# Last head's extra rows behind three known own rows, spread over three groups; 17 row dots per head instead of 16

## What is computed

```
q = (hc @ wq) -> [token, 8 heads, 2, 128];  sc = q . keys        (128 keys per half)
s1,i1 = top_k(sc[...,0], 16); s2,i2 = top_k(sc[...,1], 16)
top,pos = top_k(s1[:,None] + s2[None,:], 16); eidx = i1*128 + i2; gate = softmax(top)
act = gelu(u_tab[eidx] . hc);   out = sum_k (gate * act) * v_tab[eidx]
```

## Time and profile before

| what | value |
|---|---|
| median of 3 runs | 3503.8 us (3500.09 to 3504.2) |
| the profiled execution | 3505.83 us |
| its span | 3504.1 us |
| PE, DVE busy | 3398.9 us (97%), 2943.3 us (84%) |
| ACT, POOL busy | 1369.3 us (39%), 958.6 us (27%) |

### The profile page before, as it was taken

One profiled execution on the slowest core, in us unless ns is written; L12 is line 12 of the kernel. 1 busy time (PEld: TensorE's weight loads), 2 busy tenths in 40 slices (PEclk: granted clock), 3 DMA queues, 4 the chain that ended last, 5 costly groups with the idle time before them and its releaser, 6 DMA issues. The chain is left out here.

```text
span 3504.1 us, 67960 instructions
## 1 busy us (share of the span) xinstructions
PE 3398.9 (97%) x27550; PEld 3113.1 (89%) x27550; DVE 2943.3 (84%) x5651; ACT 1369.3 (39%) x2116; POOL 958.6 (27%) x756
## 2 busy tenths in 40 slices
PE   8899899999999999999999989999999999999998
PEld 5678777899999999999997877789999999999997
DVE  8687574899999978888888757489999997888887
ACT  3542353433334443333344234343333444333333
POOL 2000000044453333444510000003445333333352
PEclk9999999999999999999999999999999999999999
DMA  7830432499999999999962043249999999999995
GB/s 233 295 105 28 128 121 67 148 327 344 325 377 311 347 317 348 379 381 377 368 229 84 12 131 111 76 131 334 347 321 376 313 349 317 365 378 384 375 365 203
DMA packets 392169, 922.19 MB, mean 263 GB/s; under 512 B 33968, under 2 KB 211248, under 8 KB 385072
## 3 DMA queue, kind: packets, MB, share of 16 engines
q1 hardware_dynamic: 298672, 582.20, 48.6%
q0 software_dynamic: 93184, 335.65, 25.4%
HBM read 802.51 MB, written 113.05 MB: 261 GB/s over the span
## 5 line engine op out<-in xcount | busy, mean ns | idle before, releaser
L2570 POOL DMA_INDIRECT row<-in_peer_u_rows,row_at x320 | 424.4, 1326 | 654.2 <-DVE row L2908 574.3
L228 PE MATMUL peer_ps<-peer_h_high,tile_high 128*128 128x352 f32 (+1 forms) x1504 | 496.4, 330 | 6.3 <-DVE tile_low L221 6.2
L229 PE MATMUL peer_ps<-peer_h_low,tile_high 128*128 128x352 f32 (+1 forms) x1504 | 492.1, 327 | 0.0
L230 PE MATMUL peer_ps<-peer_h_high,tile_low 128*128 128x352 f32 (+1 forms) x1504 | 491.5, 327 | 0.0
L221 DVE TENSOR_TENSOR tile_low<-peer_tile,tile_high 128x1024 fp32r<-128x1024 f32 x362 | 439.6, 1215 | 27.2 <-ACT tile_high L216 26.9
L228 PE MATMUL peer_ps<-gate_high,tile_high 128*128 128x352 f32 x1360 | 441.0, 324 | 2.4 <-DVE tile_low L221 2.3
L230 PE MATMUL peer_ps<-gate_high,tile_low 128*128 128x352 f32 x1360 | 441.5, 325 | 0.0
L229 PE MATMUL peer_ps<-gate_low,tile_high 128*128 128x352 f32 x1360 | 439.6, 323 | 0.0
L216 ACT ACTIVATE tile_high<-peer_tile 128x1024 fp32r<-128x1024 f32 x362 | 379.8, 1050 | 80.6 <-DMA peer_tile<-in_peer_u 75.6
L216 ACT ACTIVATE gate_high<-weighed 128x352 fp32r<-128x352 f32 x256 | 127.8, 499 | 619.0 <-DMA peer_tile<-in_peer_v 301.8
L2908 DVE SCALAR_TENSOR_TENSOR row<-row,h_own 128x1024 f32<-128x1024 f32 x256 | 308.7, 1218 | 14.7 <-DMA row<-in_peer_u_rows,row_at 14.6
(11 more groups left out here) (569 smaller groups left out, 8042.7 us busy)
## 6 DMA issues: line engine op xcount, KB each, us to landing
peer_tile<-in_peer_u SPq DMA_DIRECT2D x256, 512.0 KB, 6.3
peer_tile<-in_peer_v SPq DMA_DIRECT2D x256, 512.0 KB, 6.2
gates<-gates_out SPq DMA_DIRECT2D x44, 1024.0 KB, 9.1
gates_in<-gates SPq DMA_DIRECT2D x32, 1408.0 KB, 10.0
acts<-up_act SPq DMA_DIRECT2D x220, 176.0 KB, 6.9
act_in<-acts SPq DMA_DIRECT2D x220, 176.0 KB, 6.4
in_w<-in_w_in SPq DMA_DIRECT2D x32, 512.0 KB, 3.6
peer_tile<-in_peer_wq SPq DMA_DIRECT2D x32, 512.0 KB, 4.5
```

What stands on the lines that cost most here:

```text
L228: pe.matmul(out, wh, mh, start=first, stop=False)
L229: pe.matmul(out, wh, ml, start=False, stop=False)
L230: return pe.matmul(out, wl, mh, start=False, stop=last)
L2570: pool.indirect_dma_start(row_of(n)[:, :], None, table, bass.IndirectOffsetOnAxis(ap=row_at[:, row_col(n):row_col(n) + 1], axis=0)) \
```

## The change

It sets `ROWS_BY_HEAD` to 17, `ROWS_BY_TILE` to 1.25 and `DOTS_UNTIL` to 4. The last head's part of the row order puts three own rows of earlier heads in front of the four extra rows. In the groups the cumulative number of rows is at least 1, 2 and 3 after the first three groups. The positions of the gate placing, part gathers, stations and one part sum follow.

```diff
-ROWS_BY_HEAD, ROWS_BY_GROUP, ROWS_BY_TILE = 16, 0.75, 1.5
-DOTS_UNTIL = 8
+ROWS_BY_HEAD, ROWS_BY_GROUP, ROWS_BY_TILE = 17, 0.75, 1.25
+DOTS_UNTIL = 4
@@ row_order
-        first = min(hd * TOPK, own + ROWS_BY_HEAD // 2) if hd + 1 < PH else own
+        first = min(hd * TOPK, own + ROWS_BY_HEAD // 2) if hd + 1 < PH else own + 3
@@
-PART_GATES_AT = (71, 119)
-PART_GATHER_AT = {48: 0, 89: 1, 100: 2, 108: 3, 122: 4, 125: 5, 128: 6, 131: 7}
-PART_STATIONS_AT = ({5: (0, 1), 6: (2,), 7: (3,)}, (3, 6, 9, 13), ((4,), (5,), (6,), (7,)))
+PART_GATES_AT = (75, 126)
+PART_GATHER_AT = {51: 0, 94: 1, 106: 2, 114: 3, 129: 4, 132: 5, 135: 6, 138: 7}
+PART_STATIONS_AT = ({5: (0, 1), 6: (2,), 7: (3,)}, (4, 6, 9, 13), ((4,), (5,), (6,), (7,)))
-PART_SUMS_IN_SPREAD = {0: 3, 4: 4, 8: 5, 11: 6, 15: 7}
+PART_SUMS_IN_SPREAD = {0: 3, 5: 4, 8: 5, 11: 6, 15: 7}
@@ peer, vector
-                rows(searched_rows + 4 + int(ROWS_BY_GROUP * (g + 1)))
+                rows(searched_rows + 4 + max(min(g + 1, 3), int(ROWS_BY_GROUP * (g + 1))))
```

## The result

Before 3504.0 us (3500.09 to 3505.63, 4 runs), after 3529.16 us (3523.91 to 3533.89, 4 runs): ratio 1.0072, 95% interval 1.0052 to 1.0092. The change makes the kernel slower by 25 us. The forecast was 3505.7 with a range to 3516; the time lies above the whole range.

A forecast was written before the change was run, and what follows sets the result against it. PE was taken to set the pace by a small margin over DVE, except at the bridge, where DVE waits for gathers. Search +12.8, bridge -6.9 and tail -4.0 gave +1.9 on 3503.8, so 3505.7 us; range 3493 to 3516.

The forecast's parts named there:

- Seven more rows in the search: Search phase: seven more row dots on DVE, six in heads 2 to 7 costing 6.9 us a layer before idle fills.
- the first gaps: Search, heads 1 and 2: a row in each first gap waits for its gather, costing 1.0 and 1.7 us a layer.
- The stall at r0: Search, first gap of head 1: DVE stands 2.9 us until r0's gather lands at 696.9, at a cost of 1.0 us.
- r20: Search, first gap of head 2: this extra row is wanted before its gather lands, a stall of 1.7 us.
- The bridge: From search to groups: known rows first remove PE's 3.25 and 2.75 us waits at tile 102 and the slow clock, -6.9 us.
- the landing of r122: Bridge: this extra row, wanted fourth, lands by about 1070.6, so low 102 is ready when PE needs it.
- The tail: Tail before the down phase: fewer rows and later gathers end PE's waits, -4.0 us of 4.7, bounds -4.7 and 0.
- Fewer rows in the down phase, first add at tile 6 instead of 10: Down phase: costs nothing, as PE does not wait for these rows now; bounds -1 and +1 us.
- The rule on one DMA: Gathers of 512 KB: 2.0 us plus bytes over 436 GB/s, 3.2 us; by it the sum is about -3.5 us.
- The rivals: DVE absorbs search rows 3493.9 (0.23); prompt landings 3500.3 (0.06); late r0 and r20 3517.1 (0.14); no bridge gain 3512.6 (0.15).
- The chance of 0.27 on slower: Whole kernel: chance of a time over 3510.8 us, from late r0 and r20 and most of no bridge gain.

The follow-up runs named there:

- e11: Kernel after with DOTS_UNTIL = 8 and the row in the first gap of heads 1 and 2 put in the next gap: 3510.88 us, ratio 1.0012.
- e1: Kernel before with DOTS_UNTIL = 4 for 8 alone: 3537.5 us, ratio 1.0093.
- e2: Kernel after with DOTS_UNTIL back at 8: 3509.37 us, ratio 1.0009.
- e3: Kernel before with ROWS_END = 128 for 124, so 128 adds over 118 tiles from tile 10: 3528.38 us, ratio 1.0061.
- e5: Kernel after with ROWS_END = 120, so double adds every 8th tile at 14, 22 and on: 3547.43 us, ratio 1.0121.
- e6: Kernel before with its double adds moved four tiles ahead, start, end and number the same: 3544.6 us, ratio 1.0114.
- e9: Kernel after, adds still from tile 6, its ten double adds in step with the slab loads (18, 26, ... 90): 3500.21 us, ratio 0.9991.
- e12: Kernel before with only the change's bridge part, and all fourteen double adds in step with the slab loads (18 to 122): 3496.34 us, ratio 0.9975.
- e7: Kernel before without the loads of gate slabs 2 to 15 of each layer: 3494.86 us, ratio 0.9968.
- e8: Kernel before with ROWS_END = 128 and without the loads of gate slabs 2 to 15: 3497.95 us, ratio 0.9987.
- e10: Kernel before with the bridge part, 1.25 rows per tail tile (13 row dots left for the down phase) and fourteen double adds in step: 3496.43 us, ratio 0.9973.

## Why the prediction was wrong

- *Seven more rows in the search*, +12.8 with the first gaps: right in sum (+12.2), split +4.4 and +7.8 instead of +6.1 and +6.7. The stall at r0 was forecast at 2.9 us and was 3.49 and 2.8. At r20, forecast at 1.7 us, the first layer had none and the second 3.1. Whether the phase is longer by the stalls or by the seven dots e11 leaves open, so of this part only the total is borne out.
- *The bridge*, -6.9: the right mechanism, too large a gain. Waits and clock were taken as gone; the clock is, but 2.3 us of PE's wait stay. The failed number is the landing of r122, which was set by 1070.6 on the clock before. Moved by the 4.3 us by which DVE comes later (1069.16 against 1064.87 at L3109) that is 1074.9; DVE had it at 1076.53. The known rows didn't help as thought, since they too land 2 us and more apart. The groups took 2.9 us back, where 2.4 were counted.
- *The tail*, -4.0: PE's 4.7 us of waits are all gone. The other 2.9 us of the -7.6 lie in the mark, which is DVE's: it reaches `weigh(0)` earlier against PE, and the down phase begins with that lead. Read with the down phase, the two are +13.5.
- *Fewer rows in the down phase, first add at tile 6 instead of 10*, **0, bounds -1 and +1**: the step that failed, by 21 us between these marks, 18 without the lead that the tail hands on. It argued from a mean, "DVE has 3.85 us per tile for about 3.3 us of work", and took PE's freedom from waits in the trace before as a property of the phase. That freedom was not whole either: the trace before has 2.5 us of waits in the first layer, whose down phase is 3.7 us longer than the second's. The runs showed it to be one of an arrangement: from 3050 to 3400 the down phase moves 376 GB/s before at a DMA share of 0.99 (361 and 0.97 after), a slab load makes the tile behind it late, and whether DVE absorbs that depends on where its double adds stand against the slab. The formula at L3165 moves them with `DOTS_UNTIL`, which the prediction didn't work out: ten doubles 12 tiles apart drift through all phases of an 8-tile cycle.
- *The rule on one DMA*: r0's gather was issued at 692.52 and DVE had it at 697.49, 5.0 us later. The Trainium skill, "DMA: Bandwidth & Descriptors", section "Anatomy of one DMA", gives by its figures the estimate of 3.2 us that the prediction names; the trace does not agree, as it didn't before.
- *The rivals*: none had this mechanism. The chance of 0.27 on slower stood on the search and the bridge, which behaved.

What is shown and what is read: that the phase of the doubles against the slab loads made the loss is shown by e1, e2, e3, e5, e6, e9 and e12, and that it needs the slabs by e7 and e8. How one late tile leads to the next is read from the timelines: a double before the slab, or a late tile, puts DVE behind; it catches up at 3.2 us a tile and so asks for tiles and rows faster than PE uses them; the next slab falls into that burst, and its tile comes 2 us later still. That wasn't tested by itself: each double also brings a second gather of POOL's, and no run parts DVE's lateness from the gather. Open: what of the search is stall and what is dots, and what makes e10 begin late.

## What to carry to other kernels

Where a constant feeds a formula that spreads work over a loop, write out the places that it gives before and after, and hold them against every other period of that loop; a mean of work per turn says nothing on it. A phase near the limit of its DMA queues can run without waits only because a large periodic load meets slack on the engine that sets the pace of requests, so an absence of waits there is to be costed as something that can be lost. When a part is costed at nothing, ask what it would cost if it were late once: here five to seven waits of PE a layer, up to 3.1 us, and the slow clock behind the longest. And doubles in step are not enough by themselves (e10).

## What was unexpected of the hardware

What is issued in the 10 us before a large load shows in the load behind it. With five loads of 512 KB there the next tile came after 9.4 us on average, with seven after 11.9; the tile and the large load were the same. Where DVE catches up five become seven, and the next transfer comes later. This is read from the traces of twelve kernels, not tested by itself.

The granted clock after a stand of PE, in the 5 us window behind it: 1.00 behind 1.73 us of waiting; 0.66 behind 3.11 and 0.74 behind 2.78 in the down phases after; 0.70 behind 3.25 and 0.66 behind 2.75 at tile 102 before.
